# First mixer's last products, its norm and the first feed-forward input by token halves

## The reference, cut to what matters

```python
y = jnp.concatenate([y_a, y_b, y_c], axis=-1) @ w_out[l]
x = x + gt1 * y
h = rms_norm(x, norm_ffn[l]) * (1.0 + sc2) + sh2
x = x + gt2 * conv_glu_ffn(h, ffn_w_up[l], ffn_conv_w[l], ffn_conv_b[l], ffn_w_down[l])
```

## Time and profile before

| | us |
|---|---|
| median of 3 runs | 2662.47 |
| lowest, highest | 2662.38, 2663.61 |
| profiled execution | 2664.73 |
| its span | 2662.9 |
| TensorE busy (page, part 1) | 2486.4 |
| VectorE, ScalarE, GpSimd busy | 1452.2, 876.1, 871.6 |

### The profile page before, as it was taken

How to read it: one execution, slowest core, us unless ns; L and a number is a source line. 1 busy time by engine, 2 the same in 40 slices (tenths; PEclk the granted TensorE clock), 3 DMA queues, 4 the chain that set the end, 5 groups by cost and what they waited for, 6 DMA issues and landing times.

```text
span 2662.9 us, 36956 instructions
## 1 busy us (share of the span) xinstructions
PE 2486.4 (93%) x15164; PEld 1455.5 (55%) x15164; DVE 1452.2 (55%) x1697; ACT 876.1 (33%) x1082; POOL 871.6 (33%) x494
## 2 busy tenths in 40 slices
PE   5899999999889999999998889999888999999996
PEld 2555558886445555555554556675344555555552
DVE  5764666773486630566325687355486640466413
ACT  3255422221144520445213222321155531354303
POOL 0212110000236531555215767201226532455320
PEclk7999999999989999999998889989999999999998
DMA  7611020000301133111312612300111122211311
GB/s 322 236 41 44 17 107 3 3 3 16 118 9 64 48 105 125 64 48 59 118 69 104 103 48 70 136 1 24 56 72 48 64 87 104 87 64 48 118 33 63
DMA packets 53497, 196.29 MB, mean 74 GB/s; under 512 B 5585, under 2 KB 15313, under 8 KB 50385
## 3 DMA queue, kind: packets, MB, share of 16 engines
q1 hardware_dynamic: 45552, 176.38, 19.5%
q10 hardware_dynamic: 7776, 17.56, 1.9%
HBM read 164.55 MB, written 29.36 MB: 73 GB/s over the span
## 4 chain that ended last, share of the span: by engine, by line
PE 80%; DVE 10%; issue 2%; POOL 2%; DMA 2%; ACT 2%; SPq 0%; ACTq 0%; DVEq 0%; POOLq 0%
PE pt L1138 15%; PE pt L1144 15%; PE pt L1141 15%; PE pt L1680 11%; PE pt L573 7%; PE pt L411 3%; PE pt L714 2%; PE pt L2391 2%; PE pt L2397 2%; PE pt L2394 2%; DVE work L536 1%; PE pt L344 1%; DMA work<-in_w_mod 1%; PE pt L332 1%; PE pt L397 1%
## 5 line engine op out<-in xcount | busy, mean ns | idle before, releaser
L1088 POOL TENSOR_TENSOR slots<-work,weights_rounded 128x512 bf16<-128x512 f32 (+2 forms) x234 | 420.7, 1798 | 598.5 <-ACT weights_rounded L1247 309.0
L1141 PE MATMUL pt<-work,weights_rounded 128*128 128x512 bf16 x1248 | 334.8, 386 | 0.0
L1138 PE MATMUL pt<-rounded,weights_rounded 128*128 128x512 f32 x624 | 210.1, 453 | 15.8 <-POOL slots L1088 10.2
L1138 PE MATMUL pt<-rhs_rounded,weights_rounded 128*128 128x512 f32 x624 | 210.2, 453 | 12.0 <-POOL slots L1088 7.8
L573 PE MATMUL pt<-work 64*64 64x64 f32 (+5 forms) x4512 | 208.0, 240 | 6.5 <-DVE work L536 5.5
L1138 PE MATMUL pt<-hidden_rounded,weights_rounded 128*128 128x512 f32 x704 | 207.2, 427 | 0.4
L573 PEld LDWEIGHTS pt<-work 64*64 64x64 f32 (+3 forms) x4512 | 188.7, 138 | 26.0 <-DVE work L536 7.7
L1141 PEld LDWEIGHTS pt<-work,weights_rounded 128*128 128x128 bf16 x1248 | 100.1, 99 | 169.0 <-issue 98.1
L1144 PE MATMUL pt<-hidden_rounded,slots 128*128 128x512 bf16 x704 | 179.9, 387 | 0.0
L1141 PE MATMUL pt<-slots,weights_rounded 128*128 128x512 bf16 x704 | 174.4, 381 | 0.0
L1144 PE MATMUL pt<-rounded,slots 128*128 128x512 bf16 x624 | 171.2, 390 | 0.0
(11 more groups left out here) (368 smaller groups left out, 4112.2 us busy)
## 6 DMA issues: line engine op xcount, KB each, us to landing
work<-in_w_up SPq DMA_DIRECT2D x64, 512.0 KB, 4.0
work<-in_w_down SPq DMA_DIRECT2D x32, 704.0 KB, 4.0
work<-in_w_mod SPq DMA_DIRECT2D x10, 2048.0 KB, 8.7
slots<-in_w_in SPq DMA_DIRECT2D x31, 512.0 KB, 3.6
slots<-in_w_up SPq DMA_DIRECT2D x24, 512.0 KB, 4.8
x_scratch<-work ACTq DMA_DIRECT2D x16, 512.0 KB, 2.6
work<-x_scratch SPq DMA_DIRECT2D x16, 512.0 KB, 8.0
slots<-in_w_v SPq DMA_DIRECT2D x10, 512.0 KB, 4.3
```

Of the source, the lines that this page charges most:

```text
L1088: did(pool, pool.tensor_tensor(dst, raw, high.bitcast(F32), ALU.subtract), name)
L1138: pe.matmul(out, whi[:, k * P:k * P + P], rhs_hi(k), start=first and k == ks[0], stop=False, skip_group_check=True)
L1141: pe.matmul(out, top_half(whi)[:, k * P:k * P + P], rhs_lo(k), start=False, stop=False, skip_group_check=True)
```

## The change

The 1024 tokens of the passage are taken as two halves of 512.

- The sixteen half products come first half first (`f_part(0)` to `(7)`), then the second half (`(8)` to `(15)`), each in one of eight banks. After part 9 TensorE makes the first half's token sums, after part 10 its rows.
- VectorE: adds and square sums of the first half as its products come, then those of the second half with the first half's reciprocal, scalings and low parts put between them; at the end the second half's reciprocal, scalings and low parts.
- ScalarE: the same by halves, two roots of four columns; the spill of a whole tile stays with the second half's square.
- TensorE in the feed-forward: gate tile of column 0 for the first half, as its low parts come; second half's token sums; value tile for the first half; second half's rows; then both tiles for the second half, by k.
- `pt_emptied_dve` and `pt_filled` of `f0` to `f7` now count second halves. Three new semaphores (`half_pe`, `half_dve`, `half_act`) carry the first half's hand-overs; four of the second block are merged into `act_once` and `dve_once`, and counts of `rhs_hi` move by one.

```diff
-            for m in range(8):
-                linear(pe, f"f{m}", lambda k, m=m: woc[:, m, k * P:(k + 1) * P], YC,
...
-            pe.wait_ge(E("square_sums"), 7)
-            token_sums(pe, "ss2", w(SQ2[0]), const("ones")[:, 0:1], 1)
-            token_rows(pe, "rb2", ("rstd_sqrt", 2), one_row)
-            ffn_pe(pe, 0)
+            def f_part(i):
+                h, m = divmod(i, 8)
+                if i < 8 and i % 2 == 0:
+                    claim(pe, f"f{i // 2}")
+                elif 8 <= i < 12:
+                    half_wait(pe, "dve", ("f", i - 4))
+                elif i >= 12:
+                    pe.wait_ge(E("pt_emptied_dve"), ordinal[f"f{i - 12}"])
...
+                for k in range(3):
+                    ins = pe.matmul(f_bank(i), woc[:, m, k * P:(k + 1) * P], w(YC[k])[:, half_of(h)], start=(k == 0),
+                                    stop=(k == 2))
+                ins.then_inc(E("pt_filled" if h else "half_pe"), 1)
...
+            for i in range(16):
+                f_part(i)
+                if i == 9:
+                    sums(0)
+                if i == 10:
+                    rows(0)
+            ffn_pe(pe, 0, (lambda: sums(1), lambda: rows(1)))
```

ScalarE and VectorE:

```diff
+            for m in range(8):
+                half_wait(act, "dve", ("f", m))
+                half_did(act, act.activation(w(SQ2[m])[:, first], w(X + m)[:, first], ACT.Square), "act", ("sq", m))
+            for m in range(8):
+                act.wait_ge(E("pt_emptied_dve"), ordinal[f"f{m}"])
+                act.dma_start(kept_x(0, m), w(X + m)).then_inc(E("x_spilled"), 16)
+                did(act, act.activation(w(SQ2[m])[:, second], w(X + m)[:, second], ACT.Square), "squares")
+                if m == 1:
+                    half_wait(act, "dve", "recip")
+                    half_did(act, act.activation(small(RS, 4), small(RS, 4), ACT.Sqrt), "act", "sqrt")
+                for k in {3: (0, 1), 4: (2, 3), 5: (4, 5), 6: (6,), 7: (7,)}.get(m, ()):
+                    first_hi(k)
...
             for m in range(8):
+                f_added(0, m)
+                if m > 1:
+                    f_square(0, m - 1)
+            f_square(0, 7)
+            for m in range(8):
+                f_added(1, m)
+                if m > 1:
+                    f_square(1, m - 1)
+                if m == 1:
+                    f_recip(0)
+                if 4 <= m < 7:
+                    f_low(0, 2 * m - 8)
+                    f_low(0, 2 * m - 7)
+                for k in {3: (0, 1), 4: (2, 3), 5: (4, 5), 6: (6,)}.get(m, ()):
+                    f_scaled(0, k)
+            f_square(1, 7)
+            f_scaled(0, 7)
+            f_low(0, 6)
+            f_low(0, 7)
+            f_recip(1)
+            for k in range(9):
+                if k < 8:
+                    f_scaled(1, k)
+                if k > 0:
+                    f_low(1, k - 1)
```

The feed-forward's start on TensorE:

```diff
+            if between:
+                for g in range(2):
+                    pe.wait_ge(E("ffn_w_split"), plain_job(t, 0, g) + 1)
+                    claim_first(g)
+                    plain(0, (g,), range(8), (0,), lambda k: half_wait(pe, "dve", ("lo", k)))
+                    between[g]()
+                for k in range(8):
+                    pe.wait_ge(E("rhs_split"), 8 + 8 * t + k + 1)
+                    plain(0, (0, 1), (k,), (1,))
```

More of the change, by code:

```diff
@@ new lines, in sums @@
+            def sums(h):
+                if h:
+                    pe.wait_ge(E("square_sums"), 7)
+                else:
+                    half_wait(pe, "dve", ("acc", 7))
+                for st in range(4):
+                    at = 512 * h + st * P
+                    ins = pe.matmul(f_sums(h)[:, st:st + 1], w(SQ2[0])[:, at:at + P], const("ones")[:, 0:1], start=True,
+                                    stop=True, skip_group_check=True)
+                ins.then_inc(E("pt_filled" if h else "half_pe"), 1)
@@ new lines, in rows @@
+            def rows(h):
+                if h:
+                    pe.wait_ge(E("rstd_sqrt"), 2)
+                else:
+                    half_wait(pe, "act", "sqrt")
+                for st in range(4):
+                    ins = pe.matmul(f_rows(h)[:, st * P:(st + 1) * P], one_row(4 * h + st), const("ident"), start=True,
+                                    stop=True, skip_group_check=True)
+                ins.then_inc(E("pt_filled" if h else "half_pe"), 1)
+            for i in range(16):
[4 more added lines that the diff above has]
+                    rows(0)
@@ L815, in after_core_dve, with f_added @@
             wout_dve(dve, 7)
-            for m in range(8):
[L817 to L823, removed]
+            def f_added(h, m):
+                seq = half_of(h)
+                if h:
+                    filled(dve, f"f{m}")
+                else:
+                    half_wait(dve, "pe", ("f", m))
+                ins = dve.scalar_tensor_tensor(w(X + m)[:, seq], f_bank(8 * h + m), small(MOD + 16 + m), w(XP[m])[:, seq],
+                                               ALU.mult, ALU.add)
+                if h:
+                    V_(ins, "pt_emptied_dve")
+                else:
+                    half_did(dve, ins, "dve", ("f", m))
@@ new lines, in f_square @@
+            def f_square(h, k):
+                seq = half_of(h)
+                if h:
+                    dve.wait_ge(E("squares"), 8 + k + 1)
+                    V_(dve.tensor_tensor(w(SQ2[0])[:, seq], w(SQ2[0])[:, seq], w(SQ2[k])[:, seq], ALU.add), "square_sums")
+                else:
+                    half_wait(dve, "act", ("sq", k))
+                    half_did(dve, dve.tensor_tensor(w(SQ2[0])[:, seq], w(SQ2[0])[:, seq], w(SQ2[k])[:, seq], ALU.add),
+                             "dve", ("acc", k))
@@ new lines, in f_recip, with f_scaled @@
+            def f_recip(h):
+                rs = small(RS + 4 * h, 4)
+                if h:
+                    filled(dve, "ss2")
+                else:
+                    half_wait(dve, "pe", "ss2")
+                V_(dve.tensor_scalar(rs, f_sums(h), 1.0 / D, EPS, ALU.mult, ALU.add))
+                if h:
+                    V_(dve.reciprocal(rs, rs), "rstd_recip")
+                else:
+                    half_did(dve, dve.reciprocal(rs, rs), "dve", "recip")
+            def f_scaled(h, k):
+                seq = half_of(h)
+                if k == 0:
+                    filled(dve, "rb2") if h else half_wait(dve, "pe", "rb2")
+                ins = dve.scalar_tensor_tensor(w(SQ2[k])[:, seq], w(X + k)[:, seq], small(G2 + k), f_rows(h), ALU.mult, ALU.mult)
+                if k == 7:
+                    V_(ins, "pt_emptied_dve")
+                elif h:
+                    V_(ins, "h_scaled")
+                else:
+                    half_did(dve, ins, "dve", ("scaled", k))
@@ new lines, in f_low @@
+            def f_low(h, k):
+                seq = half_of(h)
+                if h:
+                    dve.wait_ge(E("rhs_hi"), 9 + k + 1)
+                elif k < 7:
+                    half_wait(dve, "act", ("hi", k))
+                else:
+                    dve.wait_ge(E("rhs_hi"), 8 + 1)
+                ins = dve.scalar_tensor_tensor(lo(HLO, k)[:, seq], w(SQ2[k])[:, seq], small(MOD + 24 + k),
+                                               hi(H + k)[:, seq].bitcast(F32), ALU.add, ALU.subtract)
+                if h:
+                    V_(ins, "rhs_split")
+                else:
+                    half_did(dve, ins, "dve", ("lo", k))
@@ L1146, in passes, with plain @@
                 return ins
-            def plain(j, gs, ks):
+            def plain(j, gs, ks, hs=(0, 1), wait=None):
                 for g in gs:
-                    for h in range(2):
+                    for h in hs:
                         at = plain_at(j, g)
```

93 lines of the change are left out of this document (61 added, 32 removed).

## The result

| | before | after |
|---|---|---|
| median, us | 2662.43 (4 runs) | 2681.85 (4 runs) |
| lowest, highest | 2661.56, 2663.61 | 2680.69, 2682.95 |
| profiled execution, its span | 2664.73, 2662.9 | 2681.08, 2679.3 |

The ratio is 1.0073 (95% interval 1.006 to 1.0086): the change makes the kernel slower, by 19.4 us in the medians or 0.7%. The forecast was 2681.8.

A forecast was written before the change was run, and what follows sets the result against it. VectorE's chain between the first mixer's last product and the feed-forward was taken as the bound; +2.9, +2.7 clock, +10.1 turns and +3.6 turns at T3 made +19.3, 2684.0 profiled, 2681.8 median; range 2671 to 2687.

The forecast's parts named there:

- step 2: VectorE's half-wide passes: 20.7 us from 708.1, so the first half's last low part ends eleven microseconds after the last product.
- Steps 1 and 2: Mixer products by halves on TensorE, with new sums and rows of 2.5 us, then VectorE's backlog of half-wide passes.
- Step 3: GpSimd's six weight-tile passes take turns with VectorE's backlog: first half's last low part 10.1 us later, bounds 0 and 13.7.
- Step 4: TensorE behind the first half's last low part: queued sums and rows end at 754.0; low clock costs 2.7 us.
- Step 5: Second half's VectorE passes take 12.5 us from 754.1; last low part at 766.6 against 750.92.
- Step 6: GpSimd's fourth weight tile meets VectorE's eight sums behind the last low part: +3.6 us, between 0 and 4.2.
- the 2.26: The us by which the profiled execution before lay above the median shown, taken off to forecast the median.
- Rival A: GpSimd and VectorE passes mostly don't collide: +5.6, 2668.1 us with the clock down, or +2.9, 2665.4; 12%.
- B: First half's norm is through when the last product is, so the overlap works: 2656.4 to 2660 us; 4%.
- C: No change: the moved waits fall into the 7.80 us TensorE waits before the product with `T1`; 4%.

The follow-up runs named there:

- the second experiment: The changed kernel with GpSimd making only 8 of 1024 columns of its fourth weight tile, so results are wrong; 2676.91 us, ratio 1.0056.
- all the kernels but the last: The last is the halves kept, with early roundings, a later fourth weight tile, reordered TensorE products and an earlier reciprocal; 2656.9 us, 0.9988 against the kernel before.
- the first experiment: The changed kernel with GpSimd's first three weight tiles started only after the first half's last low part; 2678.27 us, ratio 1.0059.
- the fillers: The changed kernel plus unread dummy products on TensorE, 52 behind the last part and 16 before the first half's last two low parts; 2679.69 us.
- The last two kernels: The kernel before with early GpSimd roundings only, 2663.51 us; and the halves with early roundings, later fourth tile, reordered products and earlier reciprocal, 2656.9 us.
- the last four kernels: Early GpSimd roundings on the changed kernel, 2675.89 us; with second half's sums and rows first, 2666.4; on the kernel before, 2663.51; all changes together, 2656.9.

## Why the prediction was right, step by step

The direction was decided by step 2: VectorE had 11 us of passes left when the last product was in, so there was no norm of the first half to lie beside the second's products. The forecast then had to find how the passage behind it grows, and five terms were sized.

- **Steps 1 and 2 (+2.5 on the products).** The sixteen parts with the sums and rows take 43.14 us (673.77 to 716.91) instead of 41.36: +1.8. The sixteen records cost 0.11 each, not the 0.158 of the earlier trace rows, and the reason is the clock. The prediction takes that row for one at full clock, which for most of its length it was not. These are windows of before over its 48 records, which start at 624.29 and follow each other without a gap:

```profile
626.00:627.00 1.00, 1.00 (x11) 1.00 (x11) 0.43 (x2) 0.21 (x1) 0.00 (x0) 1.00 0.56 210
627.00:628.00 1.00, 1.00 (x7) 1.00 (x7) 0.00 (x0) 1.00 (x1) 0.00 (x0) 0.51 0.07 16
628.00:629.00 1.00, 1.00 (x6) 1.00 (x6) 0.24 (x2) 0.28 (x2) 0.00 (x0) 0.50 0.00 0
```

  Up to 627 the clock is 1.00 and 11 records lie in a microsecond; from then on it is 0.50 and they are 6 or 7. TensorE had done nothing but these short records for 2.7 us when it fell, and counts as busy all the time. So 0.158 is a mean over both clocks. It stood in the forecast a second time, for the second half's sums and rows: 2.6 us there, 1.7 in after. The backlog was right: the experiment without meetings has its last low part 0.3 from the forecast.
- **Step 3 (+10.1).** Measured alone, 9.9. Passes of both engines with two operands in SBUF take turns, and those with one in PSUM don't; both readings held. By the Trainium skill's rule ("SBUF — State Buffer", section "SBUF: two separate sides") the loser is blocked for a whole instruction; the sum of 719.18, which takes 0.69 by itself, ends 0.55 us behind GpSimd's pass and agrees with it but for 0.14 us.
- **Step 4.** The low clock cost 1.6, not 2.7. TensorE was at 1.2 GHz from 721 to 741.5 in after; I let it stay low for 12 of the 17 records behind the last low part, and it came back earlier. The prediction's bound of 2.7 was none, since all 17 low would be 3.6 by its own prices. From that low part to the first scaling it was 13.0 us, 14.7 in the forecast.
- **Step 5 (12.5).** 751.04 to 763.76, 12.7. The products of both halves never held VectorE.
- **Step 6 (+3.6).** From the last low part to the product with `T1` it is 45.4 before and 49.2 in after, +3.8. The meeting alone, taken away in the second experiment, gives 4.4.

The forecast for the product with `T1` was +19.3, and the trace has +17.5. Two prices were too high, that of the short records (0.7 us among the products and 0.9 in the second half's sums and rows) and that of the clock (1.1); the other terms, each off by 0.4 at most, came out 0.9 longer together. This leaves the missing 1.8. That the median was hit nevertheless has a second cause. The profiled executions differ by 16.35 us, the medians by 19.4: before's lay 2.3 above its median, after's 0.8 below. I took the 2.26 off the sum as if both executions would have had them. The 16.35 are the 17.5 of this passage, less 0.8 by which it begins later in before and less 0.3 behind the product with `T1`. Where the 2.3 of before's execution lie, the one trace of it can't tell, except that its passage begins the latest of the ten; all the kernels but the last lie 1 to 4 us further over before in the medians than their traces say, which fits it. So the mechanism and its main terms are shown, and the agreement within 0.1 us is luck.

Rival A (no collisions) is out by the trace of after, where they stretch four low parts and a sum to 2.7 or 2.8 us each, and the first experiment puts 9.9 us on them. Its median comes only 3.4 nearer to before, because the same passes are then late for TensorE. B (a gain by overlap) needed an empty VectorE at 718; it had work to 738. C (hidden in TensorE's wait) is out, as that wait is still there, 7.51 us. What the forecast did not price apart was the order on TensorE, the largest single gain found: the second half's squares were all summed at 735.6, but its sums stood behind the first half's gate tile until 743.61 and its rows behind the value tile until 749.88, and moving these two alone brought 11.4.

## What to carry to other kernels

Before splitting a norm so that one half lies beside other work, count the passes which its engine still has when that work ends; halves of a pass cost 1.56 us for 1.31 here, and the half-size passes of two halves were a backlog of 11 us that left nothing to lie beside. In an in-order queue the short reductions on which another engine waits (16 records, 2 us) go ahead of bulk products that it doesn't wait for: this alone was 11.4 of the 17.5 us. And look where a semaphore's meaning moves with a renumbering: GpSimd's start moved from before the crowded stretch into it, for 9.9 us at the first half's end.

## What the runs showed that I had not expected

- A blocked pass is cheaper than its turn: once GpSimd is through, a 512-wide pass of VectorE ends 0.55 us later, though it takes 0.69 to 0.75 by itself.
- Taking away a stretch of low clock did not shorten the passage by its length. With the fillers the clock stayed at 1.00 until just before 752 and then was at 0.50 for nearly 7 us; of the 20.5 us at the low level in after, 1.6 counted.
- TensorE's clock fell to 0.50 at 627 in before although the engine had no gap: it was running short records one behind the other.
- Executions of one kernel stand in clusters some 5 us apart. The last two kernels have them (up to 2669.47 and 2666.92), and before too: of its 29 executions beside the last four kernels six lie at 2657.2 to 2657.8, 21 at 2661.35 to 2664.96 and one each at 2659.92 and 2667.12. It is open what they are, and with five to twelve runs of a kernel, differences of 2 or 3 us between medians are not safe.
